# A two-layer hybrid decoder step: the engines' remaining loops written out as straight program

## What is computed

```python
h = rmsnorm(x, P['norm1_w'][l])
z = h @ P['w_in'][l]
# ... retention, latent attention, RG-LRU on parts of z ...
x = x + jnp.concatenate([y_ret, y_mla, y_rg], axis=-1) @ P['w_out'][l]
f, ffn_buf = conv_ffn(rmsnorm(x, P['norm2_w'][l]), ffn_buf0, P['ffn_w_up'][l], ...)
x = x + f

def conv_ffn(h, buf0, w_up, conv_w, conv_b, w_down):
    up = h @ w_up
    gate, val = up[..., :D_FF], up[..., D_FF:]
    gc, buf = causal_dwconv(buf0, gate, conv_w, conv_b)
    return (jax.nn.silu(gc) * val) @ w_down, buf
```

## Time and profile before

| what | us |
|---|---|
| three runs, median (lowest to highest) | 1603.57 (1600.98 to 1603.72) |
| the profiled execution, its time | 1601.4 |
| its span, first to last instruction | 1599.5 |
| mean granted TensorE clock over the span | 0.92 |
| PE busy with matmuls | 1401.2 (88%) |
| DVE busy | 867.8 (54%) |
| ACT busy | 532.1 (33%) |

### The profile page before, as it was taken

The page is one execution under the profiler, slowest core; times in us unless marked ns, Lnnn a source line. Parts: engine busy times, 40 slices in busy tenths (PEclk is TensorE's granted clock), DMA queues, the critical chain, the costliest instruction groups (busy, mean ns, idle before and its releaser), DMA issues. The chain is left out here.

```text
span 1599.5 us, 29336 instructions
## 1 busy us (share of the span) xinstructions
PE 1401.2 (88%) x11116; PEld 1265.1 (79%) x11116; DVE 867.8 (54%) x1443; ACT 532.1 (33%) x785; POOL 22.2 (1%) x43
## 2 busy tenths in 40 slices
PE   6987777569999999999999867775799999999996
PEld 6986433349899999999999844442598999999995
DVE  5586443343766634666656834442356665356655
ACT  4341233222534322334423313332244433233332
POOL 1001000000000000000100100000000000000000
PEclk9997778779999999999999977787899999999998
DMA  8312330342233233232353033303322332332221
GB/s 312 110 60 55 95 93 27 86 126 70 76 92 91 74 98 106 81 93 78 122 174 92 25 101 83 83 21 99 97 89 79 92 89 80 95 106 81 83 86 70
DMA packets 83204, 146.69 MB, mean 92 GB/s; under 512 B 12529, under 2 KB 45714, under 8 KB 82994
## 3 DMA queue, kind: packets, MB, share of 16 engines
q1 hardware_dynamic: 80546, 135.72, 28.9%
q0 software_dynamic: 2576, 9.84, 1.7%
HBM read 141.27 MB, written 4.45 MB: 91 GB/s over the span
## 5 line engine op out<-in xcount | busy, mean ns | idle before, releaser
L1277 PE MATMUL PS<-XNH,WH 128*128 128x260 f32 x2176 | 447.4, 287 | 39.3 <-issue 17.7
L1277 PE MATMUL PS<-XNH,WL 128*128 128x260 f32 x2176 | 443.9, 286 | 0.0
L1277 PE MATMUL PS<-XNL,WH 128*128 128x260 f32 x2176 | 443.3, 286 | 0.0
L1277 PEld LDWEIGHTS PS<-XNH,WH 128*128 128x128 f32 x2176 | 340.6, 191 | 43.4 <-issue 29.4
L464 ACT ACTIVATE WH<-RAW 128x1024 fp32r<-128x1024 f32 x200 | 211.6, 1058 | 432.3 <-PE PS L1277 381.3
L1277 PEld LDWEIGHTS PS<-XNH,WL 128*128 128x128 f32 x2176 | 339.5, 190 | 0.3
L1277 PEld LDWEIGHTS PS<-XNL,WH 128*128 128x128 f32 x2176 | 339.2, 190 | 0.4
L776 DVE TENSOR_TENSOR WL<-RAW,WH 128x1024 fp32r<-128x1024 f32 x200 | 244.4, 1222 | 166.7 <-ACT WH L464 166.6
L1277 PE MATMUL PS<-HL,WH 128*128 128x260 f32 x704 | 141.9, 283 | 0.0
L1277 PE MATMUL PS<-HH,WL 128*128 128x260 f32 x704 | 141.5, 282 | 0.0
L1277 PE MATMUL PS<-HH,WH 128*128 128x260 f32 x704 | 141.3, 282 | 0.0
(11 more groups left out here) (252 smaller groups left out, 1324.8 us busy)
## 6 DMA issues: line engine op xcount, KB each, us to landing
RAW<-in_units SPq DMA_DIRECT2D x134, 512.0 KB, 3.6
KT<-in_kat SPq DMA_DIRECT2D x256, 80.0 KB, 2.0
KA<-in_ka SPq DMA_DIRECT2D x256, 64.0 KB, 1.8
RAW<-in_units SPq DMA_DIRECT2D x32, 384.0 KB, 3.1
RAW<-in_units SPq DMA_DIRECT2D x32, 320.0 KB, 2.8
C<-in_const POOLq DMA_DIRECT2D x1, 2196.0 KB, 10.8
X<-in_x SPq DMA_DIRECT2D x8, 260.0 KB, 5.8
out_y<-YF SPq DMA_DIRECT2D x8, 260.0 KB, 2.2
```

What stands on the lines that cost most here:

```text
L1277: last = mm(PS[i % 4][0:rows, hb, 0:HB], w, x(kk)[:, hb * HB:(hb + 1) * HB], start=(kk == 0 and s == 0), stop=(kk == total - 1 and s == 2))
```

## The change

All these loops become Python loops, so that every turn stands in the program with its own constants. Conditions that asked whether an index was a number now ask for the half (`hf`). No operation on data is added, removed or put in another order on its engine; what goes is branches and register work, and the programs become longer.

```diff
@@ SP
                 two_steps(l, 0, 0, 1)
-                with sp.Fori(0, 2) as half:
+                for half in range(2):
                     two_steps(l, 0, 1, half)
-                with sp.Fori(0, 2) as grp:
-                    with sp.Fori(0, 2) as half:
+                for grp in range(2):
+                    for half in range(2):
                         two_steps(l, 1, grp, half)
...
-                    with sp.Fori(0, n // NRAW) as it:
+                    for it in range(n // NRAW):
                         for j in range(NRAW):
@@ ACT
-                    with act.Fori(0, n // 2) as it:
+                    for it in range(n // 2):
                         for jj in range(2):
...
-                        with act.Fori(0, 2) as it:
+                        for it in range(2):
                             for j in range(8):
                                 hi_down(l, hf, j, it)
@@ DVE
-                    with dve.Fori(0, n // 2) as it:
+                    for it in range(n // 2):
                         for jj in range(2):
...
-                            if isinstance(m, int) and m < KD - 1:
+                            if hf and m < KD - 1:
...
-                        with dve.Fori(0, 2) as it:
+                        for it in range(2):
                             down(it, 8)
@@ PE
-                    with pe.Fori(0, n // 2 - (hf == 0)) as it:
+                    for it in range(n // 2 - (hf == 0)):
                         for j in range(4):
                             product(l, f"up{hf}_{j}", [(U_UP[hf] + j, KD)], xh, xl, it=it, per=4, off=int(hf == 0))
-                    with pe.Fori(0, KD // 4) as it:
+                    for it in range(KD // 4):
                         wait(pe, "hl_ready", l, j0 + n)
```

## The result

| | us |
|---|---|
| after, median of 7 runs (lowest to highest) | 1591.08 (1584.06 to 1593.76) |
| before, median of 7 runs beside it | 1603.08 (1600.08 to 1604.46) |
| after / before, with 95% interval | 0.9932 [0.9915, 0.9948] |
| the same two kernels in a later session, 12 and 20 runs | 0.9940 [0.9919, 0.9962] |

The change is faster, by 10.9 us by the first ratio (8.3 to 13.6), 9.6 by the second. (The two medians of the table lie 12.0 us apart; I go by the ratio, which has an interval.) I had said 6.7. The sign was right, and so were, as will be seen, the places where the gain lies, though the pages' part came in part by another path. The size was too small: the median lies 0.9 us under the low end of the range, and the ratio, taken of the 1603.57 of the prediction, gives 1592.7, just inside it.

The account below looks back on a forecast made before the run. PE, busy 88% of the span, was taken as the bound, so savings count only where it waits. Pages 1.5 + 2.4, handoffs 1.8 and clock 1.0 make 6.7 us, from 1603.6 to 1597.0 us; range 1592.0 to 1602.5.

Parts of the forecast that it names:

- PE's loops: Output projection and feed-forward: writing out PE's loops gains nothing, taken as 0 with bounds 0 and 2 us.
- ACT's and DVE's later turns: Feed-forward loops after their first turn: no gain, because PE's run of matmuls covers their register work.
- the weights: SP's weight requests in the feed-forward: no gain, as they lie under the cover of PE's matmuls.
- Rival B: PE pauses at each fetch of its longer program, 33 packets at 0.41 us, 13.5 us slower: 1610.4 us; chance 0.08.
- Rival D: PE's 20 turns back cost a hidden 0.41 us each, so 8.2 us more gained: 1588.7 us; chance 0.02.
- The pages: SP's page requests in attention, phase 1: straight program gains 1.5 us in layer 0 and 2.4 in layer 1.
- the fetches: SP's straight page requests: one instruction-fetch pause of 0.41 us per 8 groups, 0.8 us up to dp5, 1.2 to dp7.
- Rival A: Attention: PE's wait for pages passes to ACT's softmax, leaving only the second gain of 1.8 us: 1601.8 us; chance 0.20.
- The handoffs: Head of the feed-forward, ahead of up0_2: shorter ACT and DVE handoffs gain 0.9 us a layer, 1.8 in all.
- The clock: Low granted clock after the wait ahead of up0_2: a shorter wait gains 0.5 us a layer, 1.0 in all.
- Rival C: Low clock after the shorter wait goes in both layers, 5.8 instead of 1.0 us: 1592.1 us; chance 0.10.

Follow-up runs that it names:

- e1: SP's page loops of both phases alone written out, against the kernel before: 1594.29 us, 0.9952 [0.9932, 0.9973].
- e12: SP's page loops alone written out, timed a second time, against the kernel before: 1595.75 us, 0.9978 [0.9961, 0.9996].
- e3: PE's feed-forward loops alone written out, against the kernel before: 1599.33 us, 0.9989 [0.9975, 1.0003].
- e4: SP's weight-request loops of the feed-forward alone written out, against the kernel before: 1601.89 us, 1.0002 [0.9986, 1.0017].
- e10: The early-splits kernel e7 with PE's feed-forward loops put back as loops: 1580.28 us, 0.9882 [0.9856, 0.9908] of the kernel before.
- e6: SP's loops of phase 1 (value pages) alone written out, phase 0 (key pages) left a loop, against the kernel before: 1591.86 us, 0.9944 [0.9921, 0.9967].
- e9: The early-splits kernel e7 with SP's page loops put back as loops: 1586.97 us, 0.9916 [0.9890, 0.9941] of the kernel before.
- e11: The early-splits kernel e7 unchanged, timed again beside e9 and e10: 1577.64 us, 0.9863 [0.9833, 0.9892] of the kernel before.
- e5: SP's page loops and ACT's and DVE's feed-forward loops written out, against the kernel before: 1590.97 us, 0.9944 [0.9923, 0.9966].
- e2: ACT's and DVE's feed-forward loops alone written out, against the kernel before: 1596.06 us, 0.9976 [0.9962, 0.9990].
- e8: The whole change unaltered, timed again in the session of e5 to e7: 1591.26 us, 0.9940 [0.9919, 0.9962] of the kernel before.
- e7: Early splits: whole change, plus DVE splitting up0_2's and up0_3's weights earlier in each layer's first turn, next gate's ahead of the taps later: 1582.53 us, 0.9888 of before.

## Why the prediction was right, and where it was too small

All fourteen profiled executions (before, after and e1 to e12) can be grouped by what they have. Means in us, worked out as in the table of stretches; the clock's loss is 1 less the granted clock of the 20 or 25 us around the wait, times that stretch.

| | executions | layer 0 | layer 1 |
|---|---|---|---|
| SP's 96 requests, page loops | 5 | 60.7 | 62.3 |
| the same, pages straight | 9 | 58.7 | 59.7 |
| dp0 to end of dp7, page loops | 5 | 65.7 | 67.8 |
| the same, pages straight | 9 | 64.0 | 64.7 |
| `wo` and feed-forward, ACT and DVE in loops | 6 | 437.4 | 438.4 |
| the same, straight | 4 | 436.7 | 435.3 |
| the same, early splits | 4 | 430.6 | 430.7 |
| loss by the clock, ACT and DVE in loops | 6 | 3.1 | 2.6 |
| the same, straight | 4 | 3.0 | 0.9 |
| the same, early splits | 4 | 0 | 0 |

**PE's loops, ACT's and DVE's later turns, the weights: nothing.** Right, by e3, e4, e10. Rival B's 33 pauses of PE don't exist: the 89 packets came, and the matmuls stayed at 119.8 ns (115.00 / 960). Rival D is out by e10.

**The pages: 3.9 said, 4.8 found, in part by another path.** SP's requests became 2.0 us shorter in layer 0 and 2.6 in layer 1, where 3.6 less 1.2 for the fetches, so 2.4, was said of each. The stretch of PE became 1.7 and 3.1 shorter, where 1.5 and 2.4 was said: 0.2 and 0.7 too little.

The path held only up to sample 5. The prediction had SP as the slow one "to the last page of the layer". In all nine executions with straight pages, and in both layers, SP's first request for sample 6 goes out 0.98 to 1.23 us after dp4 ends, and SP stands 0.8 to 2.9 us ahead of it, as in the rows above. With page loops the same request came 1.8 to 3.5 us after dp4. So what SP wins up to there is partly given back to a wait for PE, on average 1.5 us in layer 0 and 0.7 in layer 1 (beyond the 0.6 of the other places), and dp7, which starts 1.6 to 1.9 us after the end of SP's last request in every execution, hangs on dp4 through it. "Next late after SP is ACT's softmax" was right; that it would come in through sample 6's buffer was not seen, and that the sizes came out as near as they did is in part luck. Rival A, that the softmax takes the wait over, did not come as it was put: dp6 waits 2.52 as before, and dp5 and dp7 still wait for pages. It came in part, at dp4.

**The handoffs: 0.9 a layer said, 0.84 found** (4.13 to 3.29 us), in each of the four executions with ACT and DVE straight and no early splits, and in none of the six with them in loops. Of the four handoffs, the one ahead of GB, which was priced between two rows at 0.27 less, fell by 0.23.

**The clock: 1.0 said, 1.8 found. In proportion this is the term that was most mis-sized,** "I take 0.5 a layer, near the lower end, since the wait stays over 3 us"; the pages were short by about as many us. Behind a wait of 4.1 us the low clock always came: 12 cases, 2.8 us of loss on average. Behind one of 3.3 us it came in 6 of 8 cases, and cost 1.9 on average. By layer it is 0.1 us less in layer 0 and 1.7 in layer 1: all but none of it is in layer 1. It is not a smaller loss in each execution, but a whole one (about 3.4 us), half a one (about 1.7) or none, and which, differs from execution to execution of the same program: after has none in layer 1, in its second profile about half (0.93 over 25 us). Rival C, that it goes in both layers, holds in none of the four executions; it went in layer 1 in two of them, in layer 0 in none. That the shorter wait makes the loss rarer or shorter rests on 8 cases against 12, and is not shown beyond them. That the loss goes when the wait goes is shown by the early splits: none in 8 cases.

**The sum.** 4.8 + 1.7 + 1.8 = 8.3 us of the 10.9 (8.3 to 13.6) and 9.6 (6.1 to 13.0) that the ratios give. What is left, 1.3 to 2.6 us, is not accounted for by any term, and it lies inside the intervals. It may be the pages': five timings of theirs (e1, e6, e12, e9 against e11, e5 against e2) lie between 3.5 and 9.3 us, mostly over the 4.8 of the traces. In the profiled pair of e9 and e11, whose spans lie 8.4 us apart, 3.5 us are between dp0 and dp7, 4.3 ahead of dp0 in the two layers, and 1.5 in `wo` and feed-forward of layer 0.

The stretch from the start to dp0 of layer 0 is 1.2 us shorter on average with straight pages, but it runs from 282.6 to 287.6 us, and the granted clock goes with it more than the pages do. Over the first 280 us that clock was 0.88 in before and in e11 (283.5 and 282.6 us to dp0), 0.85 in e4 and 0.84 in e8 (287.6 and 287.5); of each of these pairs the first has page loops and the second has none. And e6, which kept phase 0's loop, has one of the shortest, 282.6. So a gain of the pages ahead of dp0 is not shown, and the rest stays open.

**The range.** Its low end took C whole and nothing beyond; C together with pages without pauses, 2.0 us better, would have given 1590.1, and the two were not taken together. Nor did C come; what carried the time there was the pages' 0.9, the clock's 0.8 and the rest that is open. And three runs of before, 1600.98 to 1603.72, looked steadier than it is: later medians of before were 1598.27 to 1603.08, with single runs from 1591.6 to 1609.2.

## What to carry to other kernels

Straight program pays where an engine's own rate of issue is on the path, as SP's in the page requests, and at the one turn in which two engines hand work to each other while PE waits; where PE has a queue of work before it, the same edit was worth nothing here, and the loops of e3 and e4 could have been kept. An engine that is made faster runs into the next thing it waits for: ask what frees its buffers, as dp4 does for sample 6's pages. Cost a wait of PE with what the granted clock does behind it, and not only by its length: taking away all of the 3.3 us at the head of the feed-forward gave 6.1 and 4.6 us of stretch (436.7 to 430.6, 435.3 to 430.7). And at such a place, moving work in the order was worth more than making every handoff shorter: e7 moves a split of 1.2 us ahead of the gate block and comes to 0.9888 of before, where the change alone came to 0.9940 in the same session.

## What the runs showed of the hardware that was not expected

The granted clock falls behind a wait of PE not in a fixed way: the same 3.3 us wait of the same program was followed by a granted clock of 0.83 (a mean of the two levels) over 20 us in layer 0 and by 1.00 over 25 us in layer 1, and in another execution by 0.93 in layer 1. And a program without any change scatters by more than 10 us: 35 runs of before in one session lie between 1591.6 and 1608.1.

SP pauses in straight program, 0.34 us each by the distance of its instructions, three times in layer 0's 24 groups, close to the one of 0.41 for 8 groups of the prediction; but a second kind of delay is as large. Single DMA issues of SP took much longer than the rest. All issues of line 338 after, 288 to 310 us (duration in ns, shortest, median, longest):

```profile
L338 SPq DMA_DIRECT2D KA<-in_ka x36: 315/316/757, 288.6 to 309.7; - x36
```

Twelve issues of line 338 in this profile took 0.75 us or more, up to 1.54. Eleven of them start within 0.6 us behind a packet in q8, PE's program, the twelfth 0.85 behind one; 89 packets of 0.6 us each would cover some 3% of the span. Before, three such issues fell among layer 1's 96 requests and one among layer 0's, which is part of why those took 63.43 and not 60.27. They are there with straight pages too: two among layer 1's 96 requests after. That PE's fetch is the cause is read from the coincidence alone; no run tested it.
